# Rotary halves of a differential attention: sixteen products on TensorE exchanged for sixty-four transfers inside the chip's memory

## Chip, cores and metric

The kernel runs on one core of one Trainium2 chip. The metric is the device time of one execution in microseconds (us); the median of several executions is compared, lower is better.

## What is computed

One program computes a stack of three layers on a sequence of 512 tokens of width 1024, all in float32. The change sits in the second layer, in a differential attention with 8 heads. Each head has two queries and two keys of 64 channels; all of them are turned by a rotary embedding before the scores are formed:

```python
def rope(x, pos):
    d = x.shape[-1]
    half = d // 2
    inv_freq = ROPE_THETA ** (-jnp.arange(half, dtype=F32) * (2.0 / d))
    ang = pos.astype(F32)[:, :, None] * inv_freq
    cos = jnp.cos(ang)[:, :, None, :]
    sin = jnp.sin(ang)[:, :, None, :]
    xf = x.astype(F32)
    x1, x2 = xf[..., :half], xf[..., half:]
    return jnp.concatenate([x1 * cos - x2 * sin, x2 * cos + x1 * sin], axis=-1).astype(x.dtype)
...
def diff_attention_group(q, k, v, pos, layer, lambdas, subln):
    q = rope(q.reshape(bsz, s, 2 * hh, d), pos).reshape(bsz, s, hh, 2, d)
    k = rope(k.reshape(bsz, s, 2 * hh, d), pos).reshape(bsz, s, hh, 2, d)
    ...
        p1 = masked_softmax(jnp.einsum('bqhd,bkhd->bhqk', q1b, k1, preferred_element_type=F32) * scale, mask)
        p2 = masked_softmax(jnp.einsum('bqhd,bkhd->bhqk', q2b, k2, preferred_element_type=F32) * scale, mask)
        return jnp.einsum('bhqk,bkhe->bqhe', p1 - lam * p2, vf)
```

So every channel is multiplied by a cosine, and its partner 32 channels away by a sine (with a minus sign in the lower half), and the two are added. The same layer has a state-space group (SSM, 16 heads scanned in chunks) before the attention; both outputs go through one output projection.

## The kernel before

Activations lie with channels on the 128 partitions and the 512 tokens along the free axis. All engines run programs written out by hand and meet at semaphores. SyncE (SP) streams the weights as 411 panels through a ring of `NS` = 5 slots (line 559). ScalarE (ACT) rounds each panel to a high part `w_hi` (`hi_to`, line 1290), GpSimd (POOL) subtracts to get the low part `w_lo` (line 588), and TensorE (PE) multiplies three times per 128-row step: high by high, high by low, low by high (`units`, lines 617 to 619; this document calls such a triple a unit). Products with 256 weight columns as the moving side are lines 638 to 640 (`token_units`).

In the two stages that matter here PE interleaves such units with the small products of a scan or an attention, by tables that give a number of items per step:

- The SSM scan has 32 steps. In step s PE makes the sums for the decay of step s+1 (`segments`, lines 933 and 935), ACT takes their exponential (line 1574), VectorE (DVE) multiplies by a mask (line 2289), and PE multiplies (line 956). `SSM_FILL` says how many fill items go beside a step. The items are the projections of the first four of the attention's head pairs' queries, keys and values (`dqk0`, `dv0`, `dqk1`, `dv1`).
- The attention has 32 steps (`attend_diff`), four for each head, with 128, 256, 384 and 512 keys. In step c PE makes the scores of step c+1 (line 970, mask line 973), DVE takes maxima (`maxima`, line 2304), ACT the exponential (line 1594), DVE normalises (lines 2338 to 2341), PE transposes (line 1015), ACT copies (line 1625). Once a head PE adds value products (line 984), a sum of squares (line 992) and a spread of the root (line 998); ACT squares and copies in between (lines 1602, 1606) and takes the root (line 1612); DVE ends the head in `head_out` (lines 2309, 1843, 1844). `DIFF_FILL` has 160 items: first `dqk2`, `dv2`, `dqk3`, `dv3`, then the projection `out2a`. What of the fill is left after step 31 runs in pieces behind the last value products, the last sum of squares and the last spread. The projection `out2b` comes next. It needs PSUM banks 0 and 1, which `out2a` used last and DVE frees in `add_gated` (line 2316).

A projected tile of 128 channels (two heads' query or key halves) goes to memory by `copy_dqkv` on ACT (line 1560), into `QD[p][:, t, :]`. Then PE makes the rotation, a product with a constant 128x128 matrix `rot64` of ones and minus ones (`rotate`, line 906), into PSUM bank 2. Then DVE makes `rope(i)`: PSUM by sine (line 2258), tile by cosine (line 2260), sum (line 2261). There are 16 tiles. Each rotation is an item of the fill. `steps_done` computes after which step a tile or a rotation is complete, and ACT and DVE take their parts one step later. After a tile's copy ACT casts a weight panel further down the ring (`hi_to`), and after tile 0 of `dqk2` it also makes the root of the SSM's norm, with two table loads (lines 1313, 1551); PE spreads that root in the fill (line 674).

`SIN` and `COS` are made once, in DVE's code for the tile group `z`.

Of the kernel before, what the change touches and what calls it, by code (L numbers as in the profile page):

```python
# [11 lines left out]
ALU = mybir.AluOpType  # L12
# [3 lines left out]
P = 128  # L16
S = 512
# [118 lines left out]
for _name, _n in LATE:  # L136
# [5 lines left out]
    ("ident", 128), ("ones", 128), ("after", 128), ("causal01", 128), ("rot64", 128), ("rot32", 128),  # L142
# [28 lines left out]
def constants():  # L171

    i = np.arange(P)
    c = {}
# [7 lines left out]
    rot = np.zeros((P, P))  # L182
    for m in range(P):
        rot[m + 32 if m % 64 < 32 else m - 32, m] = -1.0 if m % 64 < 32 else 1.0
    c["rot64"] = rot
    rot = np.zeros((P, P))
# [69 lines left out]
def build(nc, xt, weights, vectors, late, consts, masks, w_gates, positions, out):  # L256

    ctx = ExitStack()
    with ctx:
# [123 lines left out]
        VD = [area(at + 4 * S, ST, 2 * P) for at in QV_AT]  # L383
        COS, SIN = area(27648, S), area(28160, S)
# [147 lines left out]
        def dqkv_items(p):  # L532
            name = f"dqk{p}"
            return [((name, 0), 8), ((name, 1), 8), (("rot", 4 * p), 1), ((name, 2), 8), (("rot", 4 * p + 1), 1),
                    ((name, 3), 8), (("rot", 4 * p + 2), 1), (("part", p), 12), (("rot", 4 * p + 3), 1),
                    ((f"dv{p}", 0), 4)]

        SSM_FILL = (3, 3, 3, 4)
# [62 lines left out]
        def _(pe):  # L601
# [299 lines left out]
            def rotate(i):  # L901
                p, n = divmod(i, 4)
                pe.wait_ge(s_qc, i + 1)
                if i >= 1:
                    pe.wait_ge(s_rotf, i)
                mm_(ps[:, 2, :], con("rot64"), QD[p][:, n, :], start=True, stop=True).then_inc(s_rot, 1)

            def fill_dqkv(p):
                for n in range(4):
                    yield from units((f"dqk{p}", n), HX)  # L910
                    if p == 2 and n == 0:
                        norm_cols("gate", 7)
                    if p == 2 and n == 1:
                        norm_spread("gate", 7, RTG)
                    if n:
                        rotate(4 * p + n - 1)
                        yield
                for u, _ in enumerate(token_units((f"dv{p}", 0), HX)):
                    yield
                    if u == 11:  # L920
                        rotate(4 * p + 3)
                        yield
# [358 lines left out]
        def _(act):  # L1281
# [263 lines left out]
            def copy_dqkv(tile):  # L1545
# [12 lines left out]
                if name == f"dqk{p}":  # L1558
                    bank = USE[tile][0][0]
                    link(nc.scalar.copy(QD[p][:, t, :], ps[:, bank, :]))  # L1560
                    act.sem_inc(bank_free[bank], 1)
                    act.sem_inc(s_qc, 1)
                else:
                    copy_rows(tile, lambda q: VD[p][:, q, :], s_vd)
# [266 lines left out]
        def _(dve):  # L1831
# [410 lines left out]
            for t in range(8):  # L2242
                silu_input(t)
                if t == 1:
                    angles(POS, con("freq64"), ANG, ANG2, 16)
                    dve.sem_inc(s_ang, 1)
                times_dt(t)
                if t == 5:
                    dve.wait_ge(s_sin, 1)
                    cosine(COS)  # L2250
                    link(v.tensor_tensor(COS, COS, R, ALU.mult))
                    link(v.tensor_tensor(SIN, SIN, R, ALU.mult))

            def rope(i):
                p, n = divmod(i, 4)
                x = QD[p][:, n, :]
                dve.wait_ge(s_rot, i + 1)
                link(v.tensor_tensor(ROPE_T, ps[:, 2, :], SIN, ALU.mult))
                dve.sem_inc(s_rotf, 1)
                link(v.tensor_tensor(x, x, COS, ALU.mult))  # L2260
                link(v.tensor_tensor(x, x, ROPE_T, ALU.add))
# [243 lines left out]
            def rope_mla(i):  # L2505
                x = QR[:, i - 1, :] if i else OD[:, 9, :]
                tmp = S5T[0]
                dve.wait_ge(s_rot, 16 + i + 1)
# [255 lines left out]
```

## Time and profile before

| | |
|---|---|
| median of 3 executions | 2564.46 us (2559.68 to 2565.71) |
| the profiled execution, its own time | 2565.91 us |
| its span in the profile | 2564.1 us |
| PE busy | 2482.4 us, 97% of the span |
| DVE / ACT / POOL busy | 51% / 34% / 41% |
| SSM scan | from about 1178 to 1298 us of the span |
| attention with its fill | from about 1300 to 1515 us |

Busy time of PE is the union of its matmul records, which overlap, so the next start is a better measure of what a matmul takes than its own duration. The profile's chain of work is followed back from the last instruction. A row that is marked PE holds the matmul records of one float32 product twice: the product of the rotation, with both sides in plain float32, has two records.

### The profile page before, as it was taken

What the parts mean: (1) busy time and instruction counts of PE and PEld (TensorE: products, weight loads), DVE (VectorE), ACT (ScalarE), POOL (GpSimd) and SP (SyncE); (2) the same over time, 40 slices, a digit from 0 to 9 for tenths busy, and PEclk for the clock granted to TensorE, in tenths of its full rate; (3) what the DMA queues carried; (4) which work ended last, traced back from release to release, by engine and by line L of the source; (5) the groups of instructions that cost most, each with busy time, mean ns of one, the idle gap of its engine ahead of it and who ended that gap; (6) DMA issues with size and microseconds to landing.
All of it is one profiled execution on the core that took longest, in us unless ns stands there. A gap on an engine that the chain in (4) does not pass through costs nothing.

```text
span 2564.1 us, 30219 instructions
## 1 busy us (share of the span) xinstructions
PE 2482.4 (97%) x11742; PEld 1982.0 (77%) x11742; DVE 1310.1 (51%) x1960; ACT 868.5 (34%) x1360; POOL 1059.6 (41%) x830
## 2 busy tenths in 40 slices
PE   7999999999999999999989999999999889999998
PEld 6887767888888888876667778888888656788886
DVE  6336687543533321584756655596127855533301
ACT  4453345322322222334444433222224443322221
POOL 4322244544544444453222235454454222544442
PEclk9999999999999999999999999999999989999999
DMA  4212122322322233221111123232231012222232
GB/s 147 66 58 72 56 72 89 99 96 93 103 99 95 94 99 98 92 74 58 58 42 50 50 72 106 99 99 94 93 105 54 28 34 63 98 94 95 96 98 78
DMA packets 62574, 209.45 MB, mean 82 GB/s; under 512 B 6880, under 2 KB 9184, under 8 KB 62304
## 3 DMA queue, kind: packets, MB, share of 16 engines
q1 hardware_dynamic: 61424, 204.11, 24.3%
q10 hardware_dynamic: 1008, 3.41, 0.4%
q8 instruction: 94, 1.54, 0.3%
q14 instruction: 48, 0.39, 0.0%
HBM read 205.39 MB, written 2.10 MB: 81 GB/s over the span
## 4 chain that ended last, share of the span: by engine, by line
PE 86%; DVE 10%; ACT 2%; issue 1%; DMA 0%; DVEq 0%; ACTq 0%; SPq 0%
PE ps L617 24%; PE ps L619 24%; PE ps L618 24%; DVE T L2157 1%; PE ps L638 1%; PE ps L639 1%; PE ps L640 1%; PE ps L956 1%; PE ps L733 1%; ACT A L1594 1%; PE ps L725 1%; PE ps L970 1%; PE ps L984 1%; PE ps L754 1%; PE ps L756 1%
## 5 line engine op out<-in xcount | busy, mean ns | idle before, releaser
L588 POOL TENSOR_TENSOR w_lo<-w_raw,w_hi 128x512 fp32r<-128x512 f32 (+4 forms) x822 | 1049.9, 1301 | 1465.8 <-ACT w_hi L1290 1465.8
L617 PE MATMUL ps<-H,w_hi 128*128 128x512 f32 x1880 | 750.6, 399 | 22.6 <-DVEq L1852 12.9
L619 PE MATMUL ps<-H,w_lo 128*128 128x512 f32 x1880 | 736.5, 392 | 0.0
L618 PE MATMUL ps<-H,w_hi 128*128 128x512 f32 x1880 | 736.0, 391 | 0.0
L1290 ACT CAST w_hi<-w_raw 128x1024 fp32r<-128x1024 f32 (+4 forms) x411 | 403.0, 984 | 526.1 <-DMA w_raw<-in_weights_dram 519.7
L617 PEld LDWEIGHTS ps<-H,w_hi 128*128 128x128 f32 x1880 | 355.7, 189 | 110.4 <-issue 21.3
L617 PE MATMUL ps<-split,w_hi 128*128 128x512 f32 x1034 | 410.4, 397 | 6.9 <-issue 3.7
L619 PEld LDWEIGHTS ps<-H,w_lo 128*128 128x128 f32 x1880 | 355.2, 189 | 75.3
L618 PEld LDWEIGHTS ps<-H,w_hi 128*128 128x128 f32 x1880 | 355.9, 189 | 71.2 <-issue 1.7
L619 PE MATMUL ps<-split,w_lo 128*128 128x512 f32 x1034 | 404.2, 391 | 0.0
L618 PE MATMUL ps<-split,w_hi 128*128 128x512 f32 x1034 | 403.7, 390 | 0.0
L1875 DVE TENSOR_TENSOR T<-ps,R 128x512 f32<-128x512 f32 x164 | 113.4, 692 | 405.3 <-PE ps L619 400.9
L617 PEld LDWEIGHTS ps<-split,w_hi 128*128 128x128 f32 x1034 | 194.9, 189 | 49.9 <-issue 7.7
L619 PEld LDWEIGHTS ps<-split,w_lo 128*128 128x128 f32 x1034 | 194.8, 188 | 41.3
L618 PEld LDWEIGHTS ps<-split,w_hi 128*128 128x128 f32 x1034 | 195.0, 189 | 40.0 <-issue 1.4
L1882 DVE TENSOR_TENSOR X<-X,ps 128x512 f32<-128x512 f32 x48 | 33.0, 687 | 331.4 <-PE ps L619 329.8
L1304 ACT ACTIVATE SQ<-X 128x512 f32<-128x512 f32 x49 | 31.0, 632 | 211.7 <-DVEq L1884 198.7
L1477 ACT ACTIVATE T<-T 128x512 f32<-128x512 f32 x66 | 41.7, 632 | 167.7 <-DVEq L2124 167.6
L2127 DVE TENSOR_TENSOR T<-T 128x512 f32<-128x512 f32 x66 | 81.8, 1239 | 9.7
L638 PE MATMUL ps<-w_hi,H 128*128 128x256 f32 x256 | 76.9, 300 | 0.0
L639 PE MATMUL ps<-w_lo,H 128*128 128x256 f32 x256 | 72.7, 284 | 0.0
L640 PE MATMUL ps<-w_hi,H 128*128 128x256 f32 x256 | 72.6, 283 | 0.0
(408 smaller groups left out, 2423.2 us busy)
## 6 DMA issues: line engine op xcount, KB each, us to landing
w_raw<-in_weights_dram SPq DMA_DIRECT2D x323, 512.0 KB, 3.6
w_raw<-in_weights_dram SPq DMA_DIRECT2D x48, 448.0 KB, 3.2
w_raw<-in_weights_dram SPq DMA_DIRECT2D x22, 256.0 KB, 2.6
X<-in_xt_dram SPq DMA_DIRECT2D x4, 512.0 KB, 7.9
out_dram<-A SPq DMA_DIRECT2D x8, 256.0 KB, 2.1
w_raw<-in_weights_dram SPq DMA_DIRECT2D x12, 128.0 KB, 2.0
w_raw<-in_weights_dram SPq DMA_DIRECT2D x6, 192.0 KB, 2.3
A<-in_w_gates_dram ACTq DMA_DIRECT2D x1, 1024.0 KB, 4.8
```

The costliest lines, as they stand in the source:

```text
L588: sub = nc.gpsimd.tensor_tensor(w_lo[:, p % NS, c], w_raw[:, p % NS, c], w_hi[:, p % NS, c].bitcast(F32), ALU.subtract)
L617: mm_(ps[:, bank, :], r(wh), xh, start=(k == 0), stop=False)
L618: mm_(ps[:, bank, :], r(wh), xl, start=False, stop=False)
L619: mm = mm_(ps[:, bank, :], r(wl), xh, start=False, stop=(k == kt - 1))
L638: mm_(o, xh, r(wh), start=(k == 0), stop=False)
L639: mm_(o, xh, r(wl), start=False, stop=False)
L640: mm = mm_(o, xl, r(wh), start=False, stop=(k == kt - 1))
L1290: nc.scalar.copy(w_hi[:, p % NS, 0:PSIZE[p]], w_raw[:, p % NS, 0:PSIZE[p]]).then_inc(w_hi_ready[p % NS], 1)
L1477: A_(T[:, j % 2, :], T[:, j % 2, :], ACT.Silu).then_inc(s_silu, 1)
L1875: link(v.tensor_tensor(dst, ps[:, bank, :], R, ALU.mult))
L1882: link(v.tensor_tensor(X[:, t, :], X[:, t, :], ps[:, bank, :], ALU.add))
L2127: link(v.tensor_tensor(T[:, 2 + q, :], T[:, 2 + q, :], T[:, q, :], ALU.mult))
```

## The change

The rotation products go. After ACT has copied a tile, it begins four transfers from memory to memory, each moving 32 partitions by 512 floats to where the partner half lies (partitions 0 to 31 to 32 to 63, and back, and the same in the upper half of the partitions). They write to `EXCHANGED(p, t)`: for t = 0, 1, 2 a place in the area that later takes the values `VD[p]` (two slots, t = 2 takes that of t = 0 again), for t = 3 the tile `ROPE_T`. ACT waits before it begins them: for the exchange before to have landed (`s_rot`), at t = 2 and t = 3 also for a `rope` of DVE that used the place (`s_rotf`). Before the value tile is copied, it waits for the third `rope` of the group. DVE waits for 64 more of `s_rot` and makes the same three instructions, of which the first now reads two tiles of SBUF instead of one of PSUM. The sign goes into the sine table by a constant column `sign64`, with 32 columns in place of the 128 of `rot64`. The rotation items count 0 in the fill, and `SSM_FILL` falls from (3, 3, 3, 4) to (3, 3, 3, 3); `DIFF_FILL` stays.

```diff
-    ("ident", 128), ("ones", 128), ("after", 128), ("causal01", 128), ("rot64", 128), ("rot32", 128),
+    ("ident", 128), ("ones", 128), ("after", 128), ("causal01", 128), ("sign64", 32), ("rot32", 128),
...
-    rot = np.zeros((P, P))
-    for m in range(P):
-        rot[m + 32 if m % 64 < 32 else m - 32, m] = -1.0 if m % 64 < 32 else 1.0
-    c["rot64"] = rot
+    c["sign64"] = np.repeat(np.where(i % 64 < 32, -1.0, 1.0)[:, None], 32, axis=1)
...
+        EXCHANGED = lambda p, n: VD2[p][:, n % 2, :] if n < 3 else ROPE_T
+        VD2 = [area(at + 4 * S, 2, S) for at in QV_AT]
...
-            return [((name, 0), 8), ((name, 1), 8), (("rot", 4 * p), 1), ((name, 2), 8), (("rot", 4 * p + 1), 1),
-                    ((name, 3), 8), (("rot", 4 * p + 2), 1), (("part", p), 12), (("rot", 4 * p + 3), 1),
+            return [((name, 0), 8), ((name, 1), 8), (("rot", 4 * p), 0), ((name, 2), 8), (("rot", 4 * p + 1), 0),
+                    ((name, 3), 8), (("rot", 4 * p + 2), 0), (("part", p), 12), (("rot", 4 * p + 3), 0),
                     ((f"dv{p}", 0), 4)]
...
-        SSM_FILL = (3, 3, 3, 4)
+        SSM_FILL = (3, 3, 3, 3)
...
-            def rotate(i):
-                p, n = divmod(i, 4)
-                pe.wait_ge(s_qc, i + 1)
-                if i >= 1:
-                    pe.wait_ge(s_rotf, i)
-                mm_(ps[:, 2, :], con("rot64"), QD[p][:, n, :], start=True, stop=True).then_inc(s_rot, 1)
...
-                    if n:
-                        rotate(4 * p + n - 1)
-                        yield
-                for u, _ in enumerate(token_units((f"dv{p}", 0), HX)):
-                    yield
-                    if u == 11:
-                        rotate(4 * p + 3)
-                        yield
+                yield from token_units((f"dv{p}", 0), HX)
...
                     act.sem_inc(s_qc, 1)
+                    if t == 2:
+                        act.wait_ge(s_rotf, 4 * p + 1)
+                    if t == 3 and p:
+                        act.wait_ge(s_rotf, 4 * p)
+                    if 4 * p + t:
+                        act.wait_ge(s_rot, 64 * (4 * p + t))
+                    for b in range(4):
+                        to = 32 * (b ^ 1)
+                        act.dma_start(EXCHANGED(p, t)[to:to + 32, :], QD[p][32 * b:32 * b + 32, t, :]).then_inc(s_rot, 16)
                 else:
+                    act.wait_ge(s_rotf, 4 * p + 3)
                     copy_rows(tile, lambda q: VD[p][:, q, :], s_vd)
...
-                    link(v.tensor_tensor(SIN, SIN, R, ALU.mult))
+                    link(v.scalar_tensor_tensor(SIN, SIN, con("sign64")[:, 0:1], R, ALU.mult, ALU.mult))
...
-                x = QD[p][:, n, :]
-                dve.wait_ge(s_rot, i + 1)
-                link(v.tensor_tensor(ROPE_T, ps[:, 2, :], SIN, ALU.mult))
+                x, other = QD[p][:, n, :], EXCHANGED(p, n)
+                dve.wait_ge(s_rot, 64 * (i + 1))
+                link(v.tensor_tensor(other, other, SIN, ALU.mult))
+                link(v.tensor_tensor(x, x, COS, ALU.mult))
+                link(v.tensor_tensor(x, x, other, ALU.add))
                 dve.sem_inc(s_rotf, 1)
-                link(v.tensor_tensor(x, x, COS, ALU.mult))
-                link(v.tensor_tensor(x, x, ROPE_T, ALU.add))
                 dve.sem_inc(s_roped, 1)
```

The change moves instructions at two places that the prediction speaks of. The first is ACT in step 1 of the attention, where tile 0 of `dqk2` is copied (L1560 before, L1546 in the change) and the root of the SSM's norm follows it (`cols`). Before:

```order
L1625 COPY A<-ps 128x128 [waits a_own,probs_turned]
L1560 COPY A<-ps 128x512 [waits gemm_done]
L1290 CAST w_hi<-w_raw 128x1024 [waits a_own,w_loaded4]
L1313 ACT_TABLE_LOAD
L1313 ACTIVATE cols<-ps,C_ 128x4 [waits token_sums_ready]
L1551 ACT_TABLE_LOAD
L1594 ACTIVATE A,small<-ps,small 128x384 [waits probs_turned,max_ready]
```

The change:

```order
L1621 COPY A<-ps 128x128 [waits a_own,probs_turned]
L1546 COPY A<-ps 128x512 [waits gemm_done]
L1557 DMA A<-A 32x512 [waits a_own,rotated]
L1557 DMA A<-A 32x512 x3
L1276 CAST w_hi<-w_raw 128x1024 [waits w_loaded4]
L1299 ACT_TABLE_LOAD
L1299 ACTIVATE cols<-ps,C_ 128x4 [waits token_sums_ready]
L1537 ACT_TABLE_LOAD
L1590 ACTIVATE A,small<-ps,small 128x384 [waits probs_turned,max_ready]
```

The four transfers stand between the copy and the cast, ahead of the table loads, the root and the next exponential.

The second place is PE behind the last transposes (L1015, in the change L1001) and value products (L984, in the change L970) of the attention. `split4096` to `split7680` are the operands of `out2a`, `split22528` is one of `out2b`. Before, from the last of the three units behind the value products on:

```order
L619 MATMUL ps<-split5120_6657,w_lo_49 128x512
L992 MATMUL ps<-C_,T 128x1 x4
L617 MATMUL ps<-split5632_6663,w_hi 128x512
L618 MATMUL ps<-split1536_4850,w_hi 128x512
L619 MATMUL ps<-split5632_6663,w_lo_49 128x512
L617 MATMUL ps<-split6144_3955,w_hi 128x512
L618 MATMUL ps<-split2048_4855,w_hi 128x512
L619 MATMUL ps<-split6144_3955,w_lo_49 128x512
L617 MATMUL ps<-split6656_3960,w_hi 128x512
L618 MATMUL ps<-split2560_4860,w_hi 128x512
L619 MATMUL ps<-split6656_3960,w_lo_49 128x512
L998 MATMUL ps<-C_,cols 128x128 x4
```

The change:

```order
L1001 MATMUL ps<-C_,A 128x128 x4
L970 MATMUL ps<-A 128x512
L970 MATMUL ps<-A 128x384
L970 MATMUL ps<-A 128x256
L970 MATMUL ps<-A 128x128
L978 MATMUL ps<-C_,T 128x1 x4
L984 MATMUL ps<-C_,cols 128x128 x4
L617 MATMUL ps<-split22528_9678,w_hi 128x512
L618 MATMUL ps<-split21504_6710,w_hi 128x512
L619 MATMUL ps<-split22528_9678,w_lo_49 128x512
```

Eight units of `out2a` that stood here (three behind the value products, three behind the sum of squares, two behind the spread) have moved ahead, one into each place of a rotation; the three small groups now follow each other.

## Rows read from the trace of the kernel before

**Rows 1.** The page: busy times of the engines, and the chain that ended last.

```profile
PE 2482.4 (97%) x11742; PEld 1982.0 (77%) x11742; DVE 1310.1 (51%) x1960; ACT 868.5 (34%) x1360; POOL 1059.6 (41%) x830
...
PE 86%; DVE 10%; ACT 2%; issue 1%; DMA 0%; DVEq 0%; ACTq 0%; SPq 0%
```

**Rows 2.** Busy us by stretch: length, PE, PEld, DVE, ACT, POOL, clock, DMA share, GB/s.

```profile
1178.00:1298.00 120.00, 119.54 (x650) 82.87 (x649) 77.32 (x121) 52.50 (x95) 32.72 (x23) 1.00 0.14 45
1322.00:1500.00 178.00, 172.61 (x942) 128.04 (x941) 117.88 (x265) 85.72 (x211) 45.76 (x35) 1.00 0.16 51
...
1300.00:1318.00 18.00, 14.81 (x60) 11.72 (x61) 8.13 (x19) 4.39 (x14) 2.71 (x2) 0.81 0.18 59
```

**Rows 3.** Waits of PE, 1322 to 1440 (total, times, longest); one in its timeline.

```profile
PE ps L970 <- ACTq L1596: 4.3, 5, 1.7
...
1356.34 0.49 PE L970 MATMUL ps<-A 64*128 64x128 f32 x4 [0.70 <-ACTq L1596]
```

**Rows 4.** Timeline of PE without and with a rotation (start us, duration us, what).

```profile
1203.98 0.40 PE L619 MATMUL ps<-H,w_lo 128*128 128x512 f32 x1
1204.31 0.65 PE L956 MATMUL ps<-T,A 128*64 128x256 f32 x4
...
1218.22 0.39 PE L619 MATMUL ps<-H,w_lo 128*128 128x512 f32 x1
1218.45 1.02 PE L906 MATMUL ps<-A,C_ 128*128 128x512 f32 x2
1219.40 0.65 PE L956 MATMUL ps<-T,A 128*64 128x256 f32 x4
```

**Rows 5.** Transfers begun by ACT and by SP at the program's start, timelines.

```profile
8.46 0.34 ACTq L1324 DMA_DIRECT2D C_<-in_consts_dram  x1
...
2.15 1.78 SPq L562 DMA_DIRECT2D X<-in_xt_dram  x3
```

**Rows 6.** Timeline of ACT: the exponential behind a tile copy, in each stage.

```profile
1210.43 1.05 ACT L1574 ACTIVATE T<-ps,small 128x384 f32<-128x384 f32 x2 [0.50 <-PE ps L935]
...
1394.62 0.58 ACT L1594 ACTIVATE A<-ps,small 128x384 f32<-128x384 f32 x1 [1.42 <-DVE small L2305]
```

**Rows 7.** Timelines of DVE and PE: mask product of step 9 and its reader.

```profile
1212.26 1.87 DVE L2289 TENSOR_TENSOR T<-T,A 128x384 f32<-128x384 f32 x2
...
1215.71 0.87 PE L956 MATMUL ps<-T,A 128*64 128x384 f32 x4
```

**Rows 8.** Timelines of ACT and of PE in step 1 of the attention.

```profile
1323.03 0.58 ACT L1594 ACTIVATE A<-ps,small 128x384 f32<-128x384 f32 x1 [0.44 <-DVE small L2305]
...
1321.80 1.06 PE L674 MATMUL ps<-C_,cols 128*128 128x128 f32 x8
```

**Rows 9.** Timelines of PE and of ACT at the attention's end.

```profile
1504.88 0.47 PE L617 MATMUL ps<-split,w_hi 128*128 128x512 f32 x1
...
1507.04 0.95 PE L992 MATMUL ps<-C_,T 128*128 128x1 f32 x8
...
1514.68 0.50 PE L617 MATMUL ps<-split,w_hi 128*128 128x512 f32 x1 [1.53 <-DVEq L2317]
...
1505.87 0.58 ACT L1606 COPY T<-ps 128x512 f32<-128x512 f32 x1
...
1508.76 0.20 ACT L1613 ACTIVATE cols<-cols 128x4 f32<-128x4 f32 x1
```

**Rows 10.** DVE's `rope`, its three lines (duration ns min/median/max, first and last start).

```profile
L2258 DVE TENSOR_TENSOR A<-ps,A x16: 677/684/692, 1201.8 to 1432.3; 128x512 f32<-128x512 f32 x16
...
L2260 DVE TENSOR_TENSOR A<-A x16: 691/693/1744, 1202.6 to 1433.2; 128x512 f32<-128x512 f32 x16
...
L2261 DVE TENSOR_TENSOR A<-A x16: 691/693/1703, 1203.3 to 1433.9; 128x512 f32<-128x512 f32 x16
```

**Rows 11.** Timeline of PE ahead of the stretch with a low clock.

```profile
1308.23 0.70 PE L970 MATMUL ps<-A 64*128 64x256 f32 x4 [2.91 <-ACTq L1596]
```

**Rows 12.** The page: issues and landing, the smallest loads (us to landing at the end).

```profile
w_raw<-in_weights_dram SPq DMA_DIRECT2D x12, 128.0 KB, 2.0
```

More of the change, by code:

```diff
@@ L2507, in rope_mla @@
                 tmp = S5T[0]
-                dve.wait_ge(s_rot, 16 + i + 1)
+                dve.wait_ge(s_rot, 64 * 16 + i + 1)
                 link(v.tensor_tensor(tmp, ps[:, 3, :], SINM, ALU.mult))
```

## The prediction

> **What bounds the kernel.** I read the page first: PE is busy for 97% of the span and holds 86% of the chain that ended last [rows 1]. Next I cut out the stages in which rotations stand. In the SSM scan PE is busy 119.54 of 120 us; in the attention 172.61 of 178 us, while DVE and ACT have 66% and 48% [rows 2]. So PE bounds both, the scan wholly, the attention with some idle time. What ends that idle time I took from the waits: PE stood five times before the scores of a step, 4.3 us together, each time for ACT's exponential of the step before [rows 3]. That exponential needs DVE's maxima, and these stand behind DVE's normalising and `rope`. So from step 1 to step 7 (1322 to 1356 us), and once later, DVE and ACT together set the pace. PE time taken out there is not all gained.
>
> **What goes.** From the last matmul of a unit to the scan's product, start to start, it takes 0.33 us without a rotation and 1.18 us with one [rows 4]. So a rotation costs PE 0.85 us, and 16 cost **13.6 us**. Both stages are laid out by counts of items. In the scan the table itself shrinks, and I take the 8 rotations there at full value, 6.8 us. In the attention the table stays: each rotation's place goes to a unit (three matmuls 0.23 us apart, 1218.22 to 1218.45 is one [rows 4], so 0.69 us). Steps gain only 0.16 us each there, 1.3 us for eight, and the eight units are missing at the end.
>
> **The attention's end.** Before, 9.8 us pass from the first unit behind the last value products (1504.88) to the second unit of `out2b`, which had waited 1.53 us for a bank (1514.68) [rows 9]; one unit of `out2b` lies within it, so 9.1 us are spent. In the change the three small groups must wait for ACT. Its second copy ends at 1505.87 + 0.58, 1.57 us after the value products. The sum of squares takes 0.81 us (to the next start, 1507.85). The root ends at 1508.96, held up by two panel casts that stay where they are, so 4.08 us after the value products [rows 9]. Then comes the spread at 0.8 us: about 5.0 us in all. The bank wait goes too, because the last tile of `out2a` is now complete a step earlier and DVE frees its bank before it ends the head. Gain 4.1 us. Steps and end give 5.4 us of the 6.8 us of these eight rotations: **1.4 us lost**.
>
> **What comes: issues on ACT.** 64 transfers, four behind each copy. One alone takes ACT 0.34 us, three in a row took SP 1.78 us, 0.59 each [rows 5]. I take 0.4, so 1.6 us an exchange (1.4 to 2.4). Queued behind them on ACT are a panel cast (the ring is four panels ahead, no cost), and the next exponential. What hides them is ACT's idle time before it: 0.50 us in the scan's step 8, 1.42 us in the attention's step 13 [rows 6]; the other places have as much or more, except the one below. Where 1.1 us stick out in the scan, the reader is still not there: DVE is busy with `rope` until 1212.26 anyway, its product ends at 1214.13, and PE takes it at 1215.71, 1.6 us later [rows 7]. One rotation fewer leaves that margin near 0.7. I allow 0.8 us for the scan as a whole.
>
> One place has no cover: step 1 of the attention, where the four issues stand ahead of two table loads, the root and the exponential. ACT idles only 0.44 us before that exponential, and PE takes the spread root (L674) as soon as it is there [rows 8]. **Loss 1.6 us**. In the other seven exchanges of the attention the idle time covers the issues, mostly because DVE's `rope` now falls into the same steps.
>
> **DVE.** The three instructions stay, but the first one reads two tiles in SBUF now. With a PSUM operand it took 677 to 692 ns in all 16 cases; of the 32 with both operands in SBUF, eight took about 1.7 us, the longest 1.74 [rows 10]. So 16 x 8/32 x 1.0 = 4 us more on DVE. It reaches PE only where DVE sets the pace, four `rope`s of 16: **1.0 us**. The Trainium skill's "SBUF — State Buffer" (Who interferes with whom) says that a DVE instruction with two SBUF inputs contends with a GpSimd instruction that reads SBUF and that the loser blocks fully. The trace agrees. It is the rule that speaks against this change. If by that rule every first instruction were blocked for the 1.0 us that a blocked one loses here, the four that count would cost 4 us, and the gain would be 3 us smaller.
>
> `rope` also moves a step ahead in the attention (to steps 2, 8, 12, 14, 16, 18), so that it more often precedes the widest maxima: 0.5 us.
>
> **Landing.** The smallest loads land 2.0 us after issue [rows 12]; an exchange is four of half that size. DVE's `rope` comes at least one exponential and one normalising after it, some 3 us, and in the scan two steps. Cost 0; with 5 us it would cost up to 2 us a time where DVE sets the pace. On an unloaded queue nothing shows that.
>
> **Clock.** After PE had idled 2.91 us before a score product [rows 11], the granted clock of the 18 us around was 0.81 [rows 2], the lower of the two levels (1.2 against 2.4 GHz) for part of it, which costs 0.19 x 18 = 3.4 us. The new end of the attention has two idle times of 1.6 and 1.5 us with only small products between them. I take half of that price: **1.7 us**.
>
> **Sum.** 13.6 - 1.4 - 0.8 - 1.6 - 1.0 - 0.5 - 1.7 = 6.6 us gained. Against the profiled execution (2565.91 us, of which 2564.1 are the span) this gives 2559.3 us. That execution stood 1.45 us above the median of 2564.46, so I forecast **2558 us** for the median. About 0.3%, or 7.7 us, is what a measurement of this kernel can tell from no change (the three executions lie 6 us apart), and 2556.8 us is that border: the forecast lies just on the near side of it.
>
> **Rivals.**
> - All is hidden and the clock stays up. Then only the end's 1.4 and step 1's 1.6 us are lost: 10.6 us gained, 2554 us. For it: PE is 99.6% busy in the scan, and the 1.53 us of idle time at the attention's end [rows 9] left the clock up. Against: PE waits five times in the attention already [rows 3]. Chance 0.28.
> - The attention gives nothing, since DVE and ACT set its pace up to step 18: the 1.3 us of its steps and another 2 us are returned as waits, with the clock loss: 2562 us. For it: the 4.3 us of waits, and `rope` twice in four steps. Chance 0.17.
> - Slower: ACT's issues become the bound of the attention. Mechanism: with both queues at work an issue takes 0.59 us or more, an exchange 2.4 us, and it stands before the exponential that the next scores need. If in all eight exchanges of the attention it comes out whole, that is 19 us; the scan loses 2 us. 13.6 - 21 - 1.7 gives 2574 us. It decides from where an exchange exceeds ACT's idle time, 1.42 us [rows 6], and that of PE. Against: SP's DMA share is low in these stages (0.14 and 0.16 [rows 2]), and DVE's `rope` delays the exponential by itself. Chance 0.10.
> - The change doesn't do what it says: the rotations were hidden in PE's time anyway and their going leaves idle time. That is excluded in the scan by 99.6%; in the attention it is the second rival.
>
> **Chances.** Forecast 0.45, the others as given. The forecast spreads over 2555.5 to 2560.5; a third of it lies beyond the border. So faster by over 0.3%: 0.28 + 0.14, 0.42. Within: the rest of the forecast and the second rival, 0.48. Slower: 0.10. The range runs from the first rival less a clock stretch won back elsewhere (2554 - 3.4, so 2551) to 2567, which takes in the second rival and half of the third's way.
>
> **What would show it.** No L906 rows, PE's start-to-start of 0.33 us at those places; in the scan 120 us become about 114. ACT rows of 0.34 to 0.6 us each in fours, and exponentials later by 0 to 1.1 us in the scan without a wait of PE behind them. PE waits 1.5 us before the spread of the SSM's root. At the end of the attention PE idles twice, about 1.6 and 1.5 us, and no longer waits for DVE's bank. The first `rope` instruction shows a maximum near 1.7 us. The forecast is wrong if DVE's `rope` waits for the transfers, if an issue takes over 0.6 us, or if the low clock comes at the attention's end twice or not at all.

## The result, and the profile after

| | before | changed |
|---|---|---|
| median | 2564.77 us (4 executions) | 2600.82 us (2597.85 to 2606.87, 4 executions) |
| ratio | | 1.0147, 95% interval 1.0135 to 1.0159 |
| span of the profiled execution | 2564.1 us | 2596.1 us |

The changed kernel is 1.5% slower. The forecast was 2558 us, with a range that ended at 2567. The page of the changed kernel, busy times and chain, beside [rows 1]:

```profile
PE 2510.3 (97%) x11710; PEld 1979.9 (76%) x11710; DVE 1299.5 (50%) x1960; ACT 867.6 (33%) x1360; POOL 1057.8 (41%) x830
...
PE 84%; DVE 11%; ACT 2%; issue 2%; DMA 0%; ACTq 0%; DVEq 0%; SPq 0%
```

PE executes 32 records fewer (the 16 rotations), is busy for 27.9 us more, and idles for only 4 us more (85.8 instead of 81.7 us of the span). So most of the loss is no wait: the matmuls themselves became slower. The groups of the page show where, first of the kernel before, then of the changed one (group, busy us, mean ns of one):

```profile
L617 PE MATMUL ps<-H,w_hi 128*128 128x512 f32 x1880 | 750.6, 399 | 22.6 <-DVEq L1852 12.9
L619 PE MATMUL ps<-H,w_lo 128*128 128x512 f32 x1880 | 736.5, 392 | 0.0
```

```profile
L617 PE MATMUL ps<-H,w_hi 128*128 128x512 f32 x1880 | 759.4, 404 | 19.8 <-DVEq L1848 11.8
L619 PE MATMUL ps<-H,w_lo 128*128 128x512 f32 x1880 | 745.8, 397 | 0.0
```

Each unit product, in code that the diff doesn't touch, takes 5 to 6 ns more. Busy times by stretch, 800 to 900 us, where PE does nothing but units, before and after (columns as in [rows 2]):

```profile
800.00:900.00 100.00, 100.00 (x443) 82.84 (x442) 38.57 (x48) 24.61 (x27) 46.28 (x37) 1.00 0.30 100
```

```profile
800.00:900.00 100.00, 100.00 (x432) 81.10 (x431) 33.16 (x45) 24.25 (x27) 45.84 (x36) 1.00 0.29 95
```

PE is full and the granted clock is 1.00 (the 2.4 GHz level) in both, yet 432 products stand where there were 443. The mean difference between the starts of neighbouring products in this stretch is 226.67 ns before and 232.4 ns after. The timeline of PE, before, then after (start us, us):

```profile
850.44 0.39 PE L618 MATMUL ps<-H,w_hi 128*128 128x512 f32 x1
850.67 0.39 PE L619 MATMUL ps<-H,w_lo 128*128 128x512 f32 x1
850.89 0.39 PE L617 MATMUL ps<-H,w_hi 128*128 128x512 f32 x1
```

```profile
850.11 0.40 PE L619 MATMUL ps<-H,w_lo 128*128 128x512 f32 x1
850.35 0.40 PE L617 MATMUL ps<-H,w_hi 128*128 128x512 f32 x1
850.59 0.40 PE L618 MATMUL ps<-H,w_hi 128*128 128x512 f32 x1
850.82 0.39 PE L619 MATMUL ps<-H,w_lo 128*128 128x512 f32 x1
```

The matmul, its operands and the clock are the same, and the share of the DMA engines nearly so (0.30 and 0.29). What differs is where the tensors lie. `sign64` has 32 columns where `rot64` had 128, so the table of constants is 96 floats narrower, and everything allocated behind it moves down by 384 bytes in each partition: `T`, `SQ`, `R`, the small tiles, `H` (the moving operand of the units) and the arena `A` with its `split` tiles (the moving operand of the others). The weight buffers are allocated ahead of it and stay. In each partition H goes from byte 81536 to 81152; modulo 256 that is from 128 to 0. The rounded weights `w_hi` start at 38016 in both kernels, `w_lo` at 17536, and both are 128 modulo 256. The slots of a weight buffer and the 512-float rows of H lie whole multiples of 256 bytes apart, so all products of a kernel that stream H see the same two places.

### The profile page after: what moved, and what is told of

It is laid out like the page before. It is cut to its first block, busy times and chain, and to the rows that moved or that the text cites. A ratio compares the mean times of both kernels' runs of the same rounds, so it can differ in the third digit from the quotient of the medians.

```text
span 2596.1 us, 30215 instructions
## 1 busy us (share of the span) xinstructions
PE 2510.3 (97%) x11710; PEld 1979.9 (76%) x11710; DVE 1299.5 (50%) x1960; ACT 867.6 (33%) x1360; POOL 1057.8 (41%) x830
## 4 chain that ended last, share of the span: by engine, by line
PE 84%; DVE 11%; ACT 2%; issue 2%; DMA 0%; ACTq 0%; DVEq 0%; SPq 0%
PE ps L617 24%; PE ps L619 24%; PE ps L618 24%; DVE T L2153 1%; PE ps L638 1%; ACT A L1590 1%; DVE T L2285 1%; PE ps L640 1%; PE ps L639 1%; PE ps L733 1%; PE ps L942 1%; PE ps L725 1%; DVE small L2300 1%; PE ps L754 1%; PE ps L756 1%
## 5 line engine op out<-in xcount | busy, mean ns | idle before, releaser
L617 PE MATMUL ps<-H,w_hi 128*128 128x512 f32 x1880 | 759.4, 404 | 19.8 <-DVEq L1848 11.8
L619 PE MATMUL ps<-H,w_lo 128*128 128x512 f32 x1880 | 745.8, 397 | 0.0
L618 PE MATMUL ps<-H,w_hi 128*128 128x512 f32 x1880 | 745.7, 397 | 0.0
L617 PE MATMUL ps<-split,w_hi 128*128 128x512 f32 x1034 | 415.8, 402 | 5.3 <-issue 3.6
L619 PE MATMUL ps<-split,w_lo 128*128 128x512 f32 x1034 | 409.6, 396 | 0.0
L618 PE MATMUL ps<-split,w_hi 128*128 128x512 f32 x1034 | 409.3, 396 | 0.0
L2123 DVE TENSOR_TENSOR T<-T 128x512 f32<-128x512 f32 x66 | 73.4, 1113 | 9.7
```

What stands on the lines that cost most here:

```text
L617: mm_(ps[:, bank, :], r(wh), xh, start=(k == 0), stop=False)
L618: mm_(ps[:, bank, :], r(wh), xl, start=False, stop=False)
L619: mm = mm_(ps[:, bank, :], r(wl), xh, start=False, stop=(k == kt - 1))
L2123: link(v.tensor_tensor(T[:, 2 + q, :], T[:, 2 + q, :], T[:, q, :], ALU.mult))
```

## The experiments

Theory one (place, P in the recorded texts): the 384 bytes cost the whole 36 us, and more. Theory two (exchange, Q there): the transfers or their issues cost it, and the slower units are a side effect of the changed traffic. The first four kernels separate them, and with them a third (R): that any other program would do it. A ratio below is to executions of the kernel before taken in the same series, whose medians lie between 2563.45 and 2564.75 us. "Start to start" is the mean difference between the starts of neighbouring products in 800 to 900 us, unless another stretch is named.

**The change with the old places** (`e1`): a table entry that nobody reads fills the gap.

```diff
-    ("pool_inv", 64), ("eps", 1), ("freq64", 1), ("freq32", 1),
+    ("space", 96), ("pool_inv", 64), ("eps", 1), ("freq64", 1), ("freq32", 1),
...
+    c["space"] = np.zeros((P, 96))
```

> The change, with 96 unused columns added to the constants, so that every tensor behind them lies where it lay before (the constants shrank by 96 columns, 384 bytes). Theory P (place): the loss comes from the shifted addresses of the operands of TensorE; then the matmuls start 226.7 ns apart again in the dense stretches (232.4 in the change) and the time is that of the exchange alone, 2555 to 2565 us. Rival Q (the exchange itself: transfers, waits, ACT's queue): 2595 to 2605 us as in the change. Rival R (the place of the instructions in memory, or another effect of a different program): also about 2600 us.

Measured: 2558.5 us (2556.72 to 2563.01, 10 executions), ratio 0.9981 (0.9972 to 0.9991) to the kernel before, which had 2563.74 us. Starts are 226.67 ns apart again. Theory one; the exchange is in this kernel as in the changed one.

**The places without the change** (`e2`): the kernel before with a `space` of 32 floats, which gives H and the arena the changed kernel's places modulo 512.

```diff
+    ("space", 32), ("pool_inv", 64), ("eps", 1), ("freq64", 1), ("freq32", 1),
```

> The kernel before with 32 unused columns (128 bytes) added to the constants, so that the tensors behind them have the addresses of the change modulo 512 bytes, rotations kept. P, if only the address modulo 512 counts: start to start 232.4 ns, about 2605 us (the change's loss of 36 us and the 7 us that the exchange was to gain). P with another period or an absolute address: unchanged or in between. Q and R: 2564 us.

Measured: 2599.32 us (2597.89 to 2606.73, 4), ratio 1.0143 (1.0126 to 1.0161). No transfer was added, no product removed, and 232.4 ns stand in the stretch above. So 32 unused floats cost as much as the whole change did. The instructions are those of the kernel before, which leaves nothing for theory R.

**Half a period** (`e3`): the change with a `space` of 32 floats, so H at 384 modulo 512 and 128 modulo 256.

> The change with 32 unused columns: H and A (operands of TensorE) start at 384 modulo 512, which is 128 modulo 256 as before, but not modulo 512. P with a period of 256 bytes: 226.7 ns and 2555 to 2565 us. P with a period of 512: another pitch, most likely slow, 2600 us. Q and R: 2600 us.

Measured: 2559.29 us (2553.64 to 2563.12, 10), ratio 0.9982 (0.9971 to 0.9994), 226.67 ns. So a shift by 256 bytes costs nothing, while e2, a shift by 128, costs the full price: the place counts modulo 256.

**Only H and the arena back** (`e4`): the change with 384 bytes directly ahead of H, so `T`, `SQ`, `R`, the masks and small tiles stay shifted.

```diff
+        sb("space", [P, 96])
         at_h = nc.sbuf_base
```

> The change with 384 unused bytes directly ahead of H, so that H and A lie as before and the tensors between the constants and H (masks, T, ACC, SQ, R, small, cols) stay shifted. P by the moving operands of TensorE: 2555 to 2565 us, 226.7 ns. P by the tiles of DVE and ACT (T, SQ, R): still 2600 us. Q and R: 2600 us.

Measured: 2557.87 us (2554.8 to 2562.64, 10), ratio 0.9975 (0.9966 to 0.9985), 226.67 ns. It is the place of H and the arena, not that of `T`, `SQ`, `R` and the small tiles.

**Which property of the place** (`f1` to `f4`, `f6`, `f7`): the kernel before with unused bytes at one or two points, all by the same edit: 128 bytes ahead of the weight buffers (f1), ahead of these and of H (f2), ahead of H and of the arena (f3), and 64, 32 or 96 bytes ahead of H (f4, f6, f7). For `f1`:

```diff
+        sb("space_w", [P, 32])
         at_w = nc.sbuf_base
         w_raw = sb("w_raw", [P, NS, SLOT])
```

> The kernel before with 128 unused bytes per partition ahead of the weight buffers: the rounded weights then start at 38144 (0 modulo 256) instead of 38016 (128), H at 81664 and the arena at 114432 (both 0 modulo 256, as in the changed kernel). Theory A, the start of the moving operand by itself decides: start to start of the dense products 232.4 ns and about 2599 us, as with the moved place alone. Theory B, the place of the moving operand against that of the weights decides: both moved by the same 128 bytes, so 226.7 ns and 2564 us.

> The kernel before with 128 unused bytes ahead of H and 128 more ahead of the arena: H starts at 81664 (0 modulo 256), the arena at 114560 (128 modulo 256, as before). If each product goes by its own moving operand, the products that stream H are at 232.4 ns and those that stream the parts of the residual out of the arena stay at 226.7 ns, and the time lies between 2564 and 2599 us; if something common to the kernel decides (the weights, the largest tensor), all are alike. By the share of the unit products whose moving operand is H I expect about 2580 us.

> The kernel before with 64 unused bytes ahead of H: H and the arena start at 192 modulo 256 (before 128, changed kernel 0). If only a start at a multiple of 256 bytes is slow, 226.7 ns and 2564 us. If only a start at 128 modulo 256 is fast, 232.4 ns and 2599 us. If the cost grows with the distance from 128, about 229.5 ns and 2581 us.

> The kernel before with 128 unused bytes ahead of the weight buffers and 128 more ahead of H: the rounded weights start at 38144 (0 modulo 256), H at 81792 and the arena at 114560 (128 modulo 256, as before, where 226.7 ns were measured). If the place of the moving operand against the weights decides, they are now 128 apart modulo 256: 232.4 ns and 2599 us. If only the pair (0, 0) and the pair (128, 128) happened to be fast for another reason, such as the place of H alone being free whenever the weights are not at 128, 226.7 ns and 2564 us.

> The kernel before with 32 unused bytes ahead of H: H and the arena lie 32 bytes off the place of before modulo 256, the weights where they were. Measured so far: 0 off 226.7 ns, 64 off 228.9 ns, 128 off 232.4 ns. If the cost goes in proportion to the distance, 227.8 ns and 2568 us; if it goes in blocks of 64 bytes, 226.7 ns and 2564 us, or 228.9 ns and 2573 us.

> The kernel before with 96 unused bytes ahead of H: H and the arena lie 96 bytes off the place of before modulo 256. If the cost goes in proportion to the distance, between 228.9 and 232.4 ns, 230.6 ns and 2586 us; if in blocks of 64 bytes, 228.9 ns and 2573 us.

Measured, with the places modulo 256, start to start, and the number of executions (the first row is the kernel before in the series of f1, f3 and f4; the distance is that of H):

| kernel | weights | H | distance | ns | us (executions) | ratio |
|---|---|---|---|---|---|---|
| before | 128 | 128 | 0 | 226.67 | 2564.75 (19) | 1 |
| changed | 128 | 0 | 128 | 232.4 | 2600.82 (4) | 1.0147 |
| f1 | 0 | 0 | 0 | 226.67 | 2563.36 (8) | 0.9992 (0.9982 to 1.0003) |
| f2 | 0 | 128 | 128 | 232.4 | 2602.55 (2) | 1.0153 (1.0124 to 1.0183) |
| f3, arena stays at 128 | 128 | 0 | 128 | 233.3 | 2588.09 (2) | 1.0091 (1.0071 to 1.0111) |
| f4 | 128 | 192 | 64 | 228.9 | 2573.0 (8) | 1.0043 (1.0031 to 1.0055) |
| f6 | 128 | 160 | 32 | 233.3 | 2602.49 (2) | 1.0153 (1.0123 to 1.0183) |
| f7 | 128 | 224 | 96 | 233.3 | 2609.14 (2) | 1.0179 (1.0138 to 1.022) |

f1 has H at 0, where the changed kernel has it, and keeps the 226.67 ns; f2 has it at 128, where the kernel before has it, and loses them. So theory A of f1 falls: what decides is the distance between the moving operand and the weights modulo 256. The price doesn't grow with the distance, as I had half expected: 32 and 96 bytes cost at least as much as 128, and 64 bytes cost 2.2 ns, under half of that. All figures that I had written down for f4, f6 and f7 missed, f6 and f7 by far; I have no rule that gives these prices, only the four of them. Nor are 232.4 and 233.3 ns told apart by the distance: the changed kernel itself has 233.3 ns in 1800 to 1900 us. f3 shows that each product goes by its own operand: from 1560 to 2030 us its products with H start every 233.2 ns and those with `split` every 226.9 ns. The groups of PE in its stretch 1800 to 1900 us, mean ns as the second number:

```profile
L620 PE MATMUL ps<-split,w_hi 128*128 128x512 f32 x130 | 50.6, 389 | 0.0
...
L620 PE MATMUL ps<-H,w_hi 128*128 128x512 f32 x18 | 7.1, 395 | 0.0
```

The Trainium skill's "TensorE: Matmul & The Clock Gate" (Step-by-step: what each phase is for) says that the stationary and the streaming operand have read ports of their own, so that loading the next weights takes nothing from the running matmul. The runs show that at this pace the relation of the two addresses matters all the same, by 6 to 7 ns of 227; why, none of them shows.

**What the exchange itself costs** (`g1` to `g3`, `h1`, `h2`, all with the old places, so all to be read against e1 and its 2558.5 us). `g3` doubles the issues by halving each transfer, and raises the counts that wait for them:

```diff
-                        act.dma_start(EXCHANGED(p, t)[to:to + 32, :], QD[p][32 * b:32 * b + 32, t, :]).then_inc(s_rot, 16)
+                        for a in (0, S // 2):
+                            act.dma_start(EXCHANGED(p, t)[to:to + 32, a:a + S // 2],
+                                          QD[p][32 * b:32 * b + 32, t, a:a + S // 2]).then_inc(s_rot, 16)
```

> The changed kernel at the place of before, with every exchange begun as eight transfers of half the columns instead of four: ScalarE's queue gets 64 issues more, 0.6 us each, so 2.4 us more of each exchange. Theory 'the issues are hidden but for the steps where attention waits for ScalarE': 2558 us plus some 2 us at the wide step and 1 us of each of the four narrow steps in which an exchange falls, 2562 us. Rival 'each issue counts': 64 x 0.6 = 38 us more, 2597 us. Rival 'all hidden': 2558 us.

Measured: 2600.99 us (2597.97 to 2605.53, 4), 42 us over e1: the rival "each issue counts" was near, my own theory far off. Waits of PE in scan and attention, 1178 to 1520 us, of g3 (total, times, longest):

```profile
PE ps L957 <- ACTq L1595: 17.5, 10, 3.9
PE ps L920 <- ACT T L1573: 15.9, 9, 2.4
PE ps L675 <- DVEq L1863: 4.7, 1, 4.7
```

and in ACT's timeline one exchange of eight (start us, us):

```profile
1202.78 5.00 ACTq L1559 DMA_DIRECT2D A<-A  x8
1207.83 1.04 ACT L1277 CAST w_hi<-w_raw 128x1024 fp32r<-128x1024 f32 x1 [5.54 <-DMA A<-A]
```

5 us of ACT's queue can't be hidden in a scan step, and PE waits for the exponential: nine times in the scan, 15.9 us together, where e1 has one such wait of 0.3 us. That raises the question for four issues, 2.44 us. `h1` answers it by taking all of them from ACT:

```diff
+                if q in due:
+                    p, t = due[q]
+                    sp.wait_ge(s_qc, 4 * p + t + 1)
...
+                    for b in range(4):
+                        to = 32 * (b ^ 1)
+                        sp.dma_start(EXCHANGED(p, t)[to:to + 32, :], QD[p][32 * b:32 * b + 32, t, :]).then_inc(s_rot, 16)
```

(`due` is the panel five behind the tile's last one; the waits for `s_rotf` and `s_rot` go along. So the transfers also start at other times than in e1, and `rope` with them.)

> The changed kernel at the place of before, with all 64 issues of the exchanges taken from ScalarE to SyncE's queue, each behind the load of the panel whose buffer came free with the tile. Theory, that ScalarE's issues cost most of what the removed products give: eight issues instead of four added 42 us, so none may take back what the four cost in waits of the scan (3.3 us), in the scores' waits (7.1 us, of them 1.7 us new), at the root (2.2 us) and in half-clock stretches (5 us over before): 2558 us become 2550 us. Rival, that four issues fit into ScalarE's idle time and only the fifth to eighth bind: 2557 us. Rival, that SyncE held up by waits loads the weights later: slower than 2558 us, with waits for the weights that the profile shows.

Measured: 2557.99 us (2555.91 to 2559.27, 9), ratio 0.9976 (0.9967 to 0.9986): by the time alone no gain over e1, as the rival had it. The other rival, weights that come later, isn't seen: in these stages PE waits for no weights. The profile shows a gain that the time hides. Waits of PE in the scan, 1178 to 1298 us, of e1 and then the waits of h1, 1178 to 1520 us:

```profile
PE ps L943 <- DVE T L2286: 3.0, 6, 0.6
PE ps L920 <- ACT T L1571: 0.3, 1, 0.3
```

```profile
PE ps L970 <- ACTq L1597: 10.5, 9, 4.8
PE ps L970 <- DVEq L2274: 3.2, 1, 3.2
...
PE ps L956 <- DVE T L2290: 0.4, 2, 0.2
```

The scan's waits for DVE fell from 3.0 to 0.4 us and the wait for the spread root (L675 in e1, 2.2 us) is gone; the scores wait 10.5 us for ACT instead of 7.5. Later, though, in a stage that neither kernel changes, the busy times of 2030 to 2220 us of e1, then h1, then the kernel before:

```profile
2030.00:2220.00 190.00, 168.95 (x934) 122.37 (x934) 121.03 (x216) 77.14 (x162) 62.57 (x63) 0.96 0.19 57
```

```profile
2030.00:2220.00 190.00, 175.07 (x888) 126.29 (x889) 114.07 (x202) 76.56 (x161) 61.93 (x63) 0.90 0.19 57
```

```profile
2030.00:2220.00 190.00, 170.28 (x909) 121.53 (x908) 118.94 (x214) 75.35 (x161) 58.59 (x60) 0.89 0.16 52
```

The granted clock is 0.96 in e1 and 0.90 in h1: part of the time at the 1.2 instead of the 2.4 GHz level. By the clock alone that is up to 190 x 0.06 = 11 us more than in e1; compared product by product, as further down, it is 7.9 us. The kernel before has 0.89, so it is e1 that stands out here, not h1. I split every execution's span into span x granted clock ("at full clock") and the rest ("lost to the clock"), and took medians:

| kernel | executions | at full clock | lost to the clock |
|---|---|---|---|
| before | 62 | 2527.7 | 35.9 |
| e1, change with old places | 10 | 2523.8 | 33.2 |
| g1, cover kept | 11 | 2522.9 | 35.8 |
| g2, issues behind the root | 6 | 2522.1 | 31.9 |
| h1, issues on SyncE | 9 | 2516.6 | 38.3 |
| h2, h1 with cover kept | 6 | 2517.7 | 35.8 |
| g3, eight issues | 4 | 2548.2 | 52.0 |

The split is rough. The clock of an execution is known to 0.001, which is 2.6 us. And it takes every stretch at the low level for a loss, though PE stands idle in part of them and loses nothing there: 13.7 of 63.3 us in e1's profile, 19.4 of 78.6 in h1's. So the profiled executions were compared product by product. Rotations left out, every kernel executes the same 11710 product records, and at each border below all have executed the same ones. The table gives how many us less than in the kernel before pass from the product at a stretch's start to the one at its end (one execution each; with a minus, more pass; the forecast's terms in the second column):

| stretch of the kernel before | forecast | e1 | g1 | g2 | h1 | h2 | g3 |
|---|---|---|---|---|---|---|---|
| scan, 1177.7 to 1298.0 | 6.0 | 2.6 | 2.7 | 2.7 | 6.2 | 6.2 | -22.5 |
| attention and its end, 1298.0 to 1560.2 | 0.6 | -1.1 | -2.5 | 1.9 | 0.8 | 0.7 | -18.7 |
| unchanged code, 2030.1 to 2220.2 | 0 | 7.8 | 2.3 | 5.3 | -0.1 | -0.5 | -0.1 |

So ACT's issues cost 5.5 us in the two stages (h1 gains 7.0 there, e1 1.5), by the split 7 us (2523.8 to 2516.6); I had expected 8 with the clock. The medians of the time show 0.5 us of it, because e1 lost less to the clock elsewhere. g3 spends 42.7 us more than e1 in the two stages. By the split 24 of its 42 us are work and waits, and at most 19 are clock.

`g1` leaves eight units for the attention's end:

```diff
-        DIFF_FILL = (12,) + (4, 5, 5, 5) * 7 + (5, 5, 5)
+        DIFF_FILL = (12,) + (4, 5, 4, 4) * 4 + (4, 5, 5, 5) * 3 + (5, 5, 5)
```

> The changed kernel at the place of before, with eight unit products fewer taken at the steps of the attention, so that eight are left for its end, as in the kernel before. Theory, that the end of the attention lost its cover: the two waits there (1.5 us and 0.6 us) and the 1.7 us of the stretch at half clock go, 2558 us become 2555 us. Rival, that the units are wanted as much at the steps: the waits at the 32 steps grow by what the end saves (eight units are 1.8 us), 2558 us, no change.

Measured: 2559.78 us (2554.46 to 2564.67, 11), ratio 0.9979 (0.997 to 0.9988). No gain. The two waits at the end went, but PE waits 1.6 us for DVE's bank there again, as before [rows 9], and in the stretch of scan and attention 20.4 us lie at the low level instead of e1's 17.0. The rival was right in the sum, though not by the waits at the steps that it named: those for ACT and for DVE's products grew by nothing (6.4 us against 7.5, and 2.9 against 3.0); one wait of 0.9 us is new.

`g2` puts the issues of `dqk2`, tile 0, behind the root:

```diff
                     root("gate", 7)
+                    exchange(2, 0)
```

> The changed kernel at the place of before, with the four issues of the first exchange of the attention moved on ScalarE from ahead of the root of the normalization to behind it. Theory, that the issues hold up the root: the wait of 2.2 us of the spreading product for it falls to nothing, and the two stretches at half clock around it (10 us together, so 5 us lost) may go; 2558 us become 2556 us by the wait alone, 2552 us with the clock. Rival: the wait moves on to the product of the scores behind it, 2558 us.

Measured: 2555.99 us (2554.4 to 2559.2, 6), ratio 0.9972 (0.996 to 0.9983). It is what the theory said without the clock, 2.5 us under e1. The 2.2 us wait for the spread is gone; one wait for ACT behind it has grown from 2.7 to 3.7 us. Product by product the two stages take 3.1 us less than in e1, at full clock 1.7 us remain, and the intervals of the two ratios overlap, so this gain is likely, not shown. The trace shows what the new place does: with the cast, the table load and the root ahead of them in the program, the four issues run on ACT's queue from 1312.84 us on, while ACT executes the cast and the table load (from 1312.77), and the exponential follows the tile's copy after 5.2 us instead of 7.6.

`h2` makes h1's edit and g1's together.

> The issues taken to SyncE and eight unit products left for the end of the attention, together. Theory: the two gains are at different places and add up, 2550 us less 3 us, 2547 us. Rival, each gives nothing: 2558 us.

Measured: 2555.48 us (2554.89 to 2558.74, 6), ratio 0.9971 (0.996 to 0.9983). Theory and rival both missed. At full clock it stands where h1 does; its 2.5 us are the clock's, and in the two stages it gains 6.9 us to h1's 7.0: keeping the cover adds nothing there. It has the lowest median of all, by less than can be told from g2's; both beat the kernel before by 8 us and the changed kernel by 45.

## Why the prediction was wrong, step by step

**The step that failed** is one that the sum doesn't have. In the part on what goes and what comes I priced the products, the issues, DVE, the landing and the clock, and said nothing of the line of the diff in which the table of constants becomes 96 columns narrower. I read it as the removal of a constant. It moves every tensor behind it, and the 384 bytes bring the moving operands of all units 128 bytes modulo 256 off the weights. Price: e2 less before, 35.6 us, against a loss of 36.05 us. Back at the old places, in e1, the loss is a gain of 5.2 us. Against e2 the changed kernel shows no gain (2600.82 and 2599.32 us, 4 executions each). Product by product it gains 1.5 us on e2 in scan and attention, as e1 does on the kernel before; by the split the clock takes 37.7 us from it and 27.3 us from e2. My rival on the slow side, issues of ACT as the bound (2574 us), isn't what happened either: e1 with the same issues takes 2558.5 us.

**The rest of the sum** can be read in e1, whose places are those of before: 2558.5 us measured, 2558 forecast. That is luck. In scan and attention, the only stages that the sum speaks of, e1's profiled execution gains 1.5 us, not 6.6 (e3 0.9, e4 1.1). Another 7.8 us (5.2, 5.9) come from a stage whose code doesn't change, by its clock. The terms one by one:

- Rotations gone (13.6 us, 6.8 of them in the scan): nothing is left of L906, and PE's busy time of the same 120 us falls from 119.54 [rows 2] to 114.38. I had named that fall as a sign of the gain. It is idle time: e1 is through the scan only 2.6 us earlier, where 6.0 were forecast. With the issues off ACT (h1) it is 6.2 us. So the price of the rotations was right, and what ACT's issues take back in the scan was not: 3.6 us instead of 0.8.

```profile
1178.00:1298.00 120.00, 114.38 (x638) 80.60 (x636) 84.73 (x122) 53.34 (x100) 32.88 (x23) 1.00 0.23 68
...
1322.00:1500.00 178.00, 170.91 (x932) 128.94 (x931) 117.19 (x261) 84.04 (x207) 44.97 (x35) 0.98 0.20 61
```

- Issues on ACT (0.4 us each taken, 1.6 an exchange, up to 2.4): 0.61 us each, 2.44 an exchange, the upper bound. My second sign of being wrong, an issue over 0.6 us, came true. The issues don't only delay the exponential but, by the trace, the cast behind them: in ACT's timeline of e1 at step 1 of the attention, to be set beside [rows 8],

```profile
1313.33 2.44 ACTq L1558 DMA_DIRECT2D A<-A  x4
1315.81 1.05 ACT L1277 CAST w_hi<-w_raw 128x1024 fp32r<-128x1024 f32 x1 [2.69 <-DMA A<-A]
...
1320.17 0.58 ACT L1591 ACTIVATE A<-ps,small 128x384 f32<-128x384 f32 x1 [0.44 <-DVE small L2302]
```

- The scan (0.8 us allowed): PE waits 3.0 us in six steps, none of them before. The margin of 1.6 us behind DVE's product [rows 7] was smaller than what the 0.8 us more per exchange and the item fewer in every fourth step took from it. With the issues off ACT (h1) 0.4 us of these waits is left, so it is mostly the issues.
- Entering the attention (no term): the first score product waits 3.2 us for DVE instead of 1.5, in h1 too. The forecast had nothing for these 1.7 us.
- Step 1 (1.6 us): 2.2 us before the spread, the 0.61 us a piece again.
- DVE (1.0 us, from 8 first instructions of 32 at 1.7 us): one of 16 was blocked, and the mean is 740 ns against 677 to 692 [rows 10], 0.9 us on all of DVE instead of 4. The groups of DVE in e1, 1178 to 1500 us (first, third and second instruction of `rope`; the middle number is the mean):

```profile
L2255 DVE TENSOR_TENSOR A<-A 128x512 f32<-128x512 f32 x16 | 11.8, 740 | 0.7
L2257 DVE TENSOR_TENSOR A<-A 128x512 f32<-128x512 f32 x16 | 11.1, 692 | 0.5
L2256 DVE TENSOR_TENSOR A<-A 128x512 f32<-128x512 f32 x16 | 11.1, 692 | 0.6
```

  The rule of the Trainium skill that I had weighed ("SBUF — State Buffer", Who interferes with whom) didn't bite here in e1 as I had feared. In h1 the same three lines have means of 984, 942 and 1074 ns, 14 us more than in e1 in all: 33 of the 48 instructions still take about their usual 684 or 692 ns, and the other 15 take 1.5 to 1.8 us. So the blocking depends on where the exchanges fall in time. By the trace GpSimd instructions run during 64% or more of each of the 15, as of e1's single slow one, and during that much of only one of the 33 fast ones. In the kernel before, though, four fast instructions of L2260 also have GpSimd beside them for over half their time, and no run takes GpSimd's instructions away, so that it is these stays likely, not shown.
- Landing (no cost): 2.1 us median in the issues of the page, and the first `rope` instruction idles 0.7 us in all 16 together. Right.

```profile
A<-A ACTq DMA_DIRECT2D x64, 64.0 KB, 2.1
```

- The attention's end (4.1 us gained, two waits of 1.6 and 1.5 us, 1.7 us of clock): the first wait is 1.53 us, the second only 0.59, as one cast stands ahead of the root instead of two. The bank wait is gone, and one stretch of 3.4 us at half the clock, 1.7 us, lies right there (granted clock 0.91 of 1500 to 1520 us). Waits in PE's timeline of e1:

```profile
1504.18 2.40 PE L971 MATMUL ps<-A 128*128 128x512 f32 x8 [1.85 <-DVEq L1842]
...
1508.11 1.02 PE L979 MATMUL ps<-C_,T 128*128 128x1 f32 x8 [1.53 <-ACTq L1604]
...
1509.72 1.16 PE L985 MATMUL ps<-C_,cols 128*128 128x128 f32 x8 [0.59 <-ACT cols L1610]
```

- The clock as a whole: I priced one stretch, at the attention's end. But between 1170 and 1560 us e1 spends 17.0 us at the low level and the kernel before 6.8, which is up to 5.1 us lost, not 1.7. In 2030 to 2220 us it is the other way round, and more comes back than that. By the medians of the split the exchange gave 3.9 us and the clock 2.7; the medians of the time differ by 5.2.

Open stays why the clock falls less often in 2030 to 2220 us in e1 (0.96) than in h1 (0.90) and the kernel before (0.89), whose code is the same there. I didn't try it.

## What to carry to other kernels

A diff that changes the width of any early tensor moves everything allocated behind it; write down the addresses of TensorE's operands before and after, modulo 256, and hold them fixed (here with unused bytes) before a change is judged. If the mean difference of starts in a full stretch of untouched matmuls differs between two kernels at the same granted clock, look at places first, not at waits. A fall of PE's busy time in a stretch is no gain by itself; compare when the same product starts. And do that stage by stage before you call an edit worthless or a forecast right: h1's 5.5 us over e1 were there, and e1 made up for them in a stage that neither edit touches.

## What the runs showed of the hardware

- The unit products (operands rounded to float32r, 128x512 moving, one weight load of 128x128 each) start, at granted clock 1.00, every 226.67 ns when moving operand and weights lie at the same place modulo 256 bytes, every 228.9 ns when 64 bytes apart, and every 232.4 to 233.3 ns when 32, 96 or 128 apart. Of the absolute places tried (f1, f2) none mattered. Distances of 32, 64 and 96 were tried with the weights at 128 alone.
- A transfer from memory to memory of 32 partitions by 2 KB costs the queue of the engine that begins it 0.61 us, ACT and SP alike (2.41 us for four on SP), 0.63 us with half the size: the price is by the issue, not by the bytes.
- From four to eight issues an exchange, the time went up by 42 us for 39 us of issues; taking all four away won 5.5 us in the two stages (7 by the split). An engine beside the critical path costs little up to its slack and everything beyond it, the clock on top.
